# Two-block transformer, one core: layer norms computed with the tokens on the partitions

## The reference, cut to what matters

```python
for l in range(2):
    h = x @ w_in[l] + b_in[l]
    ...                                   # y_lru, y_nsa from h
    mix = concat([rms_norm(y_lru, gn_lru_g[l]), rms_norm(y_nsa, gn_nsa_g[l])]) @ w_out[l]
    x = layer_norm(ALPHA * x + mix, ln1_g[l], ln1_b[l])
    x = layer_norm(ALPHA * x + peer(x, ...), ln2_g[l], ln2_b[l])

def layer_norm(x, g, b):                  # over the 1024 features of a token
    mu = mean(x); var = mean((x - mu) ** 2)
    return (x - mu) * rsqrt(var + 1e-5) * g + b
```

## Time and profile before

| | us |
|---|---|
| median of 3 runs | 3153.09 (3152.42 to 3153.7) |
| the profiled execution | 3152.62 |
| its span, first to last instruction | 3150.8 |
| PE busy | 3091.8 (98%) |
| DVE busy | 2062.8 (65%) |
| ACT busy | 1442.4 (46%) |
| mean granted TensorE clock | 0.993 |
| PE's share of the chain that ended last | 94% |

### The profile page before, as it was taken

How to read it: one execution, slowest core, us unless ns; L and a number is a source line. 1 busy time by engine, 2 the same in 40 slices (tenths; PEclk the granted TensorE clock), 3 DMA queues, 4 the chain that set the end, 5 groups by cost and what they waited for, 6 DMA issues and landing times.

```text
span 3150.8 us, 46702 instructions
## 1 busy us (share of the span) xinstructions
PE 3091.8 (98%) x15882; PEld 2575.7 (82%) x15882; DVE 2062.8 (65%) x4058; ACT 1442.4 (46%) x2307; POOL 157.7 (5%) x289
## 2 busy tenths in 40 slices
PE   7999999999999999999999999999999999999998
PEld 6688876868887688899888888878889988888887
DVE  5567752636774352899776676665289976676676
ACT  2436642435663244156344544444415634544454
POOL 3100000200000000320000000000032000000000
PEclk9999999998999999999999999999999999999999
DMA  8748896734889632433655555644243265555663
GB/s 320 254 174 309 305 347 267 283 124 174 309 301 350 235 111 82 141 101 107 194 187 190 192 190 187 193 148 145 78 142 108 96 197 187 192 190 188 192 191 121
DMA packets 167140, 614.72 MB, mean 195 GB/s; under 512 B 18752, under 2 KB 18784, under 8 KB 166096
## 3 DMA queue, kind: packets, MB, share of 16 engines
q1 hardware_dynamic: 151632, 551.62, 51.4%
q0 software_dynamic: 15360, 61.16, 5.2%
HBM read 611.66 MB, written 1.05 MB: 194 GB/s over the span
## 4 chain that ended last, share of the span: by engine, by line
PE 94%; DVE 2%; ACT 2%; DMA 1%; issue 0%; DVEq 0%; POOL 0%; ACTq 0%; SPq 0%; POOLq 0%
PE PS L1639 13%; PE PS L1640 13%; PE PS L1641 13%; PE PS L2287 11%; PE PS L1685 7%; PE PS L2247 6%; PE PS L2289 6%; PE PS L2165 4%; PE PS L2270 4%; PE PS L1699 2%; PE PS L1726 2%; PE PS L1967 2%; PE PS L2153 2%; PE PS L2016 1%; PE PS L2279 1%; PE PS L1670 1%
## 5 line engine op out<-in xcount | busy, mean ns | idle before, releaser
L1016 DVE TENSOR_TENSOR w_lo<-arena,w_hi 128x1024 fp32r<-128x1024 f32 x448 | 530.2, 1220 | 0.0
L610 ACT ACTIVATE w_hi<-arena 128x1024 fp32r<-128x1024 f32 x448 | 451.5, 1048 | 97.3 <-DMA arena<-in_v_t 76.0
L1639 PE MATMUL PS<-w_hi,pw_hi 128*128 128x512 f32 x1024 | 402.1, 393 | 2.8 <-DVE w_lo L1016 2.3
L1640 PE MATMUL PS<-w_lo,pw_hi 128*128 128x512 f32 x1024 | 401.2, 392 | 0.0
L1641 PE MATMUL PS<-w_hi,pw_lo 128*128 128x512 f32 x1024 | 398.9, 390 | 0.0
L2287 PE MATMUL PS<-x_lh,w_hi 128*128 128x512 f32 x1536 | 379.5, 389 | 0.0
L2287 PEld LDWEIGHTS PS<-x_lh,w_hi 128*128 128x128 f32 x1536 | 288.3, 188 | 59.6
L956 ACT ACTIVATE arena<-PS 128x256 f32<-128x256 f32 x192 | 73.9, 385 | 446.8 <-PE PS L2289 446.8
L1237 DVE TENSOR_TENSOR gu_lo<-raw,gu_hi 128x1024 fp32r<-128x1024 f32 x192 | 222.6, 1221 | 19.2 <-ACT gu_hi L698 19.1
L1641 PEld LDWEIGHTS PS<-w_hi,pw_lo 128*128 128x128 f32 x1024 | 192.5, 188 | 41.4
L1639 PEld LDWEIGHTS PS<-w_hi,pw_hi 128*128 128x128 f32 x1024 | 193.1, 189 | 38.7 <-issue 2.6
(11 more groups left out here) (417 smaller groups left out, 5319.0 us busy)
## 6 DMA issues: line engine op xcount, KB each, us to landing
arena<-in_u_t SPq DMA_DIRECT2D x256, 512.0 KB, 4.5
arena<-in_v_t SPq DMA_DIRECT2D x256, 512.0 KB, 3.6
raw<-in_w_gu SPq DMA_DIRECT2D x192, 512.0 KB, 5.4
arena<-in_w SPq DMA_DIRECT2D x152, 512.0 KB, 3.6
arena<-in_w_ada POOLq DMA_DIRECT2D x96, 512.0 KB, 7.1
raw<-in_w_down SPq DMA_DIRECT2D x96, 512.0 KB, 5.6
arena<-in_w_gu SPq DMA_DIRECT2D x64, 512.0 KB, 7.4
arena<-in_w_down SPq DMA_DIRECT2D x32, 512.0 KB, 5.0
```

Of the source, the lines that this page charges most:

```text
L610: A(w_hi[:, m % RING], ring[:, m % RING], ACT.Copy).then_inc(S["hi_done"], 1)
L1016: V.tensor_tensor(w_lo[:, m % RING], ring[:, m % RING], w_hi[:, m % RING].bitcast(F32), ALU.subtract)\
L1639: mm(dst, w[0], m[0], start=start, stop=False)
L1640: mm(dst, w[0], m[1], start=False, stop=False)
```

## The change

The residual is no longer added by DVE. PE turns `x` (16 transposes, `residual`) into the four banks before the products are accumulated on top of it: in NSA eight of them before the first half of the projection and eight after the wait for the second half of `mix`, in PEER all before the first `down`. So that the sum is x + y / ALPHA, what is added is scaled by 1 / ALPHA: in NSA by a bias of the Exp that makes the rms factors, in PEER by a scale of the copy of the gates; the epsilon becomes 1e-5 / ALPHA**2. In NSA the projection's operands change places: `mix` (128 tokens) is stationary and the weight slot (128 output features) moves, so that both blocks leave tokens on the partitions. DVE then reads each bank with `bn_stats`, combines with `bn_aggr`, ACT takes a square root, DVE the reciprocal and one `tensor_scalar` per bank (subtract, multiply) into `y`; PE turns `y` with 16 transposes (`normed`) and ACT applies gain and bias out of the banks. The diff, cut (comments at the side say which engine's program it is; lines in brackets sum up lines left out):

```diff
-LN_BANK = (6, 0)
+LN_TURN = ((6, 7, 4, 5), (4, 5, 6, 7))
...
-        L_ = area([("sq", (KT, T)), ("rs", (T,)), ("y", (TT, D))], 16384)
+        L_ = area([("y", (TT, D))], 16384)
+        ln_st = sb("ln_st", [P, TT, 12])
+        ln_mv = sb("ln_mv", [P, TT, 4])
+        def ln_bank(q, t, half):
+            return 2 * t + half if q else OUT_BANK[2 * half + t]
...
             def layer_norm(l, q):                                   # ScalarE
-                for j in range(4):
-                    act.wait_ge(S["ln_c"], 4 * LN[s] + j + 1)
-                    A(L_["sq"][:, 2 * j:2 * j + 2], x[:, 2 * j:2 * j + 2], ACT.Square).then_inc(S["norm_sq"], 1)
-                root(s, L_["rs"], LN_BANK[q] + 1, LN_EPS)
+                A(ln_mv[:, 0, 2:3], ones[:, 0:1], ACT.Sqrt)
+                act.wait_ge(S["ln_var"], LN[s] + 1)
+                A(ln_mv[:, :, 1], ln_mv[:, :, 1], ACT.Sqrt, bias=LN_EPS / ALPHA ** 2).then_inc(S["ln_rs"], 1)
                 for k in range(KT):
-                    act.wait_ge(S["scaled"], KT * SIDX[s] + k + 1)
-                    A(x[:, k], x[:, k], ACT.Identity, scale=..., bias=...)
+                    act.wait_ge(S["ln_t"], KT // 2 * LN[s] + k // 2 + 1)
+                    A(x[:, k], PS[:, LN_TURN[q][k // 2], T * (k % 2):T * (k % 2) + T], ACT.Identity, scale=..., bias=...)
...
-                    A(..., ACT.Exp, scale=-0.5).then_inc(S["g_rs"], 1)
+                    A(..., ACT.Exp, scale=-0.5, bias=-math.log(ALPHA)).then_inc(S["g_rs"], 1)
...
-                A(gT, PS[:, 1, 0:T], ACT.Copy)
+                A(gT, PS[:, 1, 0:T], ACT.Copy, scale=1.0 / ALPHA)
...
-                act.wait_ge(S["slot_done"], BASE_SPLIT["peer", l] + PEER_SLOTS)
-                for q in range(2):
-                    for t in range(TT):
-                        last = A(L_["y"][:, t, 512 * q:512 * q + 512], PS[:, 2 * t + q, :], ACT.Copy)
-                    last.then_inc(S["y2_ev"], 1)
...
             def layer_norm(l, q):                                   # VectorE
-                dve.wait_ge(S["ln_mu"], LN[s] + 1)
-                for j in range(4):
-                    V.scalar_tensor_tensor(x[:, 2 * j:2 * j + 2], PS[:, LN_BANK[q], 0:T]...broadcast, -1.0 / D, x[:, ...], ALU.mult, ALU.add)
-                dve.wait_ge(S["norm_rs"], SIDX[s] + 1)
-                for k in range(KT):
-                    V.tensor_tensor(x[:, k], x[:, k], L_["rs"], ALU.mult).then_inc(S["scaled"], 1)
+                order = ((0, 0), (0, 1), (1, 0), (1, 1)) if q else ((0, 0), (1, 0), (0, 1), (1, 1))
+                for i, (t, half) in enumerate(order):
+                    if q and i < 3:
+                        dve.wait_ge(S["ln_z"], 5 * l + 2 + i + 1)
+                    elif q:
+                        dve.wait_ge(S["slot_done"], BASE_SPLIT[s] + PEER_SLOTS)
+                    elif t == 0:
+                        dve.wait_ge(S["ln_z"], 5 * l + half + 1)
+                    else:
+                        dve.wait_ge(S["slot_done"], BASE[s] + W2_IN + 4 * half + 4)
+                    V.bn_stats(ln_st[:, t, 6 * half:6 * half + 6], PS[:, ln_bank(q, t, half), :])
+                    if half:
+                        dve.drain()
+                        last = V.bn_aggr(ln_mv[:, t, 0:2], ln_st[:, t])
+                last.then_inc(S["ln_var"], 1)
+                dve.wait_ge(S["ln_rs"], LN[s] + 1)
+                V.reciprocal(ln_mv[:, :, 3], ln_mv[:, :, 1])
+                dve.drain()
+                for half in range(2):
+                    for t in range(TT):
+                        V.tensor_scalar(L_["y"][:, t, 512 * half:512 * half + 512], PS[:, ln_bank(q, t, half), :],
+                                        ln_mv[:, t, 0:1], ln_mv[:, t, 3:4], ALU.subtract, ALU.mult).then_inc(S["ln_n"], 1)
+                if not q:
+                    dve.drain().then_inc(S["pair_evac"], 4)
...
-                for j in range(4):                                  # VectorE, nsa
-                    dve.wait_ge(S["slot_done"], n0 + W2_IN + 2 * j + 2)
-                    V.scalar_tensor_tensor(x[:, 2 * j:2 * j + 2], x[...], ALPHA, PS[:, OUT_BANK[j], :]..., ALU.mult, ALU.add)\
-                        .then_inc(S["pair_evac"], 1)
...
-                V.tensor_tensor(x[:], x_hi.bitcast(F32), x_lo.bitcast(F32), ALU.add)   # VectorE, peer
-                dve.drain()
-                for j in range(4):
-                    dve.wait_ge(S["y2t"], 4 * l + j + 1)
-                    V.scalar_tensor_tensor(x[...], x[...], ALPHA, PS[:, 4 + j, :]..., ALU.mult, ALU.add).then_inc(S["z2_ok"], 1)
...
-            def means(l, q, j):                                     # TensorE
-                (two 128x256 products of ones with x per call, into PS[:, LN_BANK[q], 0:T])
+            def residual(q, half):
+                for t in range(TT):
+                    for k in range(4 * half, 4 * half + 4):
+                        mm(PS[:, ln_bank(q, t, half), P * (k % 4):P * (k % 4) + P], x[:, k, P * t:P * t + P], ident,
+                           start=k % 4 == 0, stop=False, is_transpose=True, skip_group_check=True)
+            def normed(l, q):
+                filler(9, 7)
+                for k in range(KT):
+                    if k % 4 == 0:
+                        pe.wait_ge(S["ln_n"], 4 * LN[s] + 2 * (k // 4) + 2)
+                    for t in range(TT):
+                        c0 = T * (k % 2) + P * t
+                        last = nc.tensor.transpose(PS[:, LN_TURN[q][k // 2], c0:c0 + P], L_["y"][:, t, P * k:P * k + P], ident)
+                    if k % 2:
+                        last.then_inc(S["ln_t"], 1)
...
                 def out_half(i, c):
-                    for k in range(4 * c, 4 * c + 4):
-                        last = mm(PS[:, OUT_BANK[i // 2], T * (i % 2):T * (i % 2) + T], ring[:, n % RING, P * k:P * k + P], N["mix"][:, k],
-                                  start=k == 0 and i % 2 == 0, stop=k == KT - 1, skip_group_check=True)
+                    for t in range(TT):
+                        for k in range(4 * c, 4 * c + 4):
+                            last = mm(PS[:, ln_bank(0, t, i // 4), c0:c0 + P], N["mix"][:, k, P * t:P * t + P],
+                                      ring[:, n % RING, P * k:P * k + P], start=False, stop=..., skip_group_check=True)
+                        if c and t == 0 and i % 4 == 3:
+                            last.then_inc(S["ln_z"], 1)
...
                 heads(1, (0, 1))
+                residual(0, 0)
                 pe.wait_ge(S["mix2_ok"], 2 * l + 1)
...
                 pe.wait_ge(S["mix2_ok"], 2 * l + 2)
+                residual(0, 1)
                 for i in range(W2_OUT):
                     if i >= RING:
                         out_half(i, 0)
                     out_half(i, 1)
-                    if i % 2 and i > 1:
-                        means(l, 0, i // 2 - 1)
-                means(l, 0, 3)
-                for j in range(4):
-                    squares(("nsa", l), L_["sq"], j, LN_BANK[0] + 1)
-                filler(9, 2)
+                normed(l, 0)
...
-                def down(n, j, b, i=0, per=0, start=False, stop=False):
+                def down(n, j, b, i=0, per=0, stop=False):
                     (the last call signals ln_z after each of its first three banks; no call starts a bank)
+                pe.wait_ge(S["gelu_ok"], PK * l + EARLY - LATE)
+                residual(1, 0)
+                residual(1, 1)
                 for b in range(EARLY):
-                    down(n0 + b, b, b, start=b == 0)
+                    down(n0 + b, b, b)
...
                 down(n0 + PEER_SLOTS - 1, PEER_STEP - 1, PK - 1, stop=True)
-                (16 transposes of y into banks 4 to 7, means, squares, and for l = 0 nine fillers)
+                normed(l, 1)
```

More of the change, by code:

```diff
@@ L816, in rms @@
                     act.drain()
-                    A(N["rs"][:, T * q:T * q + T], N["rs"][:, T * q:T * q + T], ACT.Exp, scale=-0.5).then_inc(S["g_rs"], 1)
+                    A(N["rs"][:, T * q:T * q + T], N["rs"][:, T * q:T * q + T], ACT.Exp, scale=-0.5, bias=-math.log(ALPHA)).then_inc(S["g_rs"], 1)
                 evac(0)
@@ L1635, in _, with mm3 @@
             mm = nc.tensor.matmul
[L1637 to L1641, removed]
+            def mm3(dst, w, m, start, stop, skip=False):
+                mm(dst, w[0], m[0], start=start, stop=False, skip_group_check=skip)
+                mm(dst, w[0], m[1], start=False, stop=False, skip_group_check=skip)
+                return mm(dst, w[1], m[0], start=False, stop=stop, skip_group_check=skip)
             def filler(n, bank):
@@ L2151, in out_half @@
                     wait_slot(pe, n)
-                    for k in range(4 * c, 4 * c + 4):
-                        last = mm(PS[:, OUT_BANK[i // 2], T * (i % 2):T * (i % 2) + T], ring[:, n % RING, P * k:P * k + P], N["mix"][:, k],
-                                  start=k == 0 and i % 2 == 0, stop=k == KT - 1, skip_group_check=True)
+                    c0 = P * (i % 4)
```

(22 more changed lines are left out.)

25 lines of the change are left out of this document (4 added, 21 removed).

## The result

| | before | changed |
|---|---|---|
| median, us | 3152.76 (3150.21 to 3153.7, 4 runs) | 3126.41 (3122.49 to 3129.93, 4 runs) |
| ratio | | 0.9917, 95% interval 0.9900 to 0.9935 |
| span of the profiled execution | 3150.8 | 3124.8 |

The forecast was 3125 (3117 to 3136). The head of the changed page, to be read against the earlier trace rows: PE's busy time fell by 16 us, the span by 26. The other 10 us are waiting that went.

A forecast was written before the change was run, and what follows sets the result against it. PE, busy 3091.8 of 3150.8 us, was taken as the bound. PEER 0 8.75, PEER 1 9.1 and the NSA blocks 9.6 sum to 27.5 us off 3152.6: 3125 forecast, range 3117 to 3136.

The forecast's parts named there:

- The four gaps: At the four layer norms PE waits on a chain between engines; these gaps hold 55 us, 15.29 after the first PEER block.
- The end of the kernel: After the second PEER block, last product to last gain-and-bias tile: 7.6 us in place of 18.58; the store's 2.4 stays.
- T0: The end of the last product before a layer norm, from which the prediction timed the norm's steps.
- The upper bound of two passes: In the norms, `bn_stats` at 1.2 us apiece: 2.0 us more in each PEER, 0.85 in each NSA, 5.7 in all.
- Gain and bias: Behind each norm, ACT's eight tiles 0.49 us apart, no table load; PE never catches up, saving 0.4 us besides.
- The exchange: In NSA's projection, 128 records of 256 columns become 256 of 128, 0.111 us apart: 0.85 us more.
- Rivals 3 and 4: In the projection: records 0.125 us apart, 3132 us, 6%; or weight loads not covered, records 0.30 apart, 3222 us, 3%.
- NSA's stretch: Each NSA projection, its norm and the next block's start: 4.8 us less, twice 9.6.
- The weight slots: At the next block's start, weights were held to be no limit, SP's order and conditions being unchanged; no cost taken.
- rival 5: The next block waits for a slot or POOL load, so gaps don't shorten: 5.9 us slower up to no change; 3%.
- the last sign of being wrong: PE idling on a weight slot where it now idles on the norm; no size given.
- rival 1: After the gaps PE's clock falls to half rate for 7 us: 3.5 us at each of three, 3136 us; 7%.

The follow-up runs named there:

- `a_split`: The changed kernel with the normalising pass shared: DVE takes token tile 0, ACT token tile 1; 3124.79 us in one run, gap 4.5 us (5.5).
- `a_res2`: The changed kernel with every group of residual transposes run twice; 3133.57 us in one run.
- `a_noex`: The changed kernel with the projection's operands not exchanged (weight slot stationary again, output wrong); 3126.68 us in one run.
- `a_first`: The changed kernel with all three of POOL's loads in NSA held back until the block's first weight slot is used; 3120.72 us, ratio to before 0.9903.
- `a_nofill`: The changed kernel without the nine filler products in each layer norm; 3131.12 us, ratio to before 0.9934.

## Why the prediction was right, and where it was off

- **The four gaps.** Right in mechanism and nearly in size. After PEER 0 5.05 was forecast and 5.5 measured. The term that was mis-sized is the normalising pass. The prediction took 0.62 us a pass from DVE's adds (2.48 us for four, which is 0.60 apart and 0.68 for one); measured are 2.96 us for four, 0.72 apart and 0.80 for one. The pass has two scalars of a column each, and the row that it was read from has none; that this is the reason was not tested. `a_split` shows that this pass is what sets the gap.
- **The end of the kernel**, 7.6 us forecast and 7.66 measured to the last tile, is two misses that cancel: the first turned tiles reached ACT 0.35 us later than forecast (T0 + 3.90, not 3.55), and the eight gain-and-bias tiles took 3.76 us and not 4.04.
- **`bn_stats`**, which no row had: 0.68 taken, 0.70 measured (0.65 at its shortest). Two of four are hidden and the third nearly, and the fourth ends at T0 + 0.79 where 0.71 was forecast. One `bn_aggr` 0.21 for 0.18. The upper bound of two passes did not come.
- **Gain and bias** came 0.45 apart, faster than 0.49, without a table load. PE had no wait in it, and of the 0.4 us hoped for 0.15 and 0.4 show in the two stretches PEER a.
- **The residual**: 1.9 forecast, 1.8 measured in PEER, exposed; `a_res2` confirms it.
- **The exchange**: 0.111 forecast and 0.112 measured apart, and 0.85 forecast and 0.9 measured a block (`a_noex`). Rivals 3 and 4 fell: with 256 loads of 0.19 us in each projection, the 512 records lie 0.1117 apart, 4 ns over half of the 0.216 of a 256-column record. By the rule of the Trainium skill, "TensorE: Matmul & The Clock Gate", section "Back-to-back issue gap", that rival 3 names, they would have lain some 25 ns further apart than the columns ask, an estimate; for these float32 products the trace disagrees with it.
- **NSA's stretch** fell by 4.2 us, and with what PEER a gained behind it by 4.4 and 4.6, where 4.8 was forecast: the normalising pass again.
- **The weight slots**: this step failed. The prediction said "The next block's weights are no limit ... SP's order and conditions are unchanged" and priced POOL's earlier start at nothing. The order within SP was unchanged; the order between SP's and POOL's loads was not. NSA 1 took 2.0 us more, where 0.4 less was forecast, and `a_first` shows the cause by taking 2.5 away. It was of rival 5's kind in one block, at a fraction of its price, and close to the last sign of being wrong that the prediction named, though PE idled on the slots 14 us behind the norm and not in it.
- **The clock** stayed up, against rival 1. `a_nofill` shows that the fillers, of which the prediction said only that they cost nothing, are what kept it up in two of three gaps.

The sum: forecast 27.5, by the stretches 24.0. Of the 3.5 between, 2.4 are in NSA 1 with its slots, 0.5 in the gap after PEER 0, and 0.6 in the two NSA norms with what follows them. That the first comparison of medians gave 26.4 fits the variation of the part that the change left alone, which was 2.1 us shorter in the profiled run. The total agreed with the forecast better than its terms did, and that much is luck.

## What to carry to other kernels

A norm between two products costs what its chain of engines costs, not its work: turn the layout so that the statistics are read where the product leaves them, let all but the last bank's share lie beside the product, and split the last full pass over two engines. When a stall goes, look at what the next stage's transfers waited for: a load released by the end of the stall may now be issued ahead of the one that PE needs first, and holding it back by one slot puts it right. Read single stretches of the timeline, not totals, where the effect is smaller than the variation between runs.

## What the hardware showed that was not expected

- The order of issue decided 2.5 us, though the transfers sit in different queues. A slot of 512 KB issued 0.1 us behind the last of three large loads on POOL's queue got no packet for 3.9 us and landed after 10.7, with the second of the three. Issued 0.55 us ahead of the first, it landed after 3.9. While both queues had work, the DMA engines took as many packets from one as from the other, 162 and 160 in 6 us, and as POOL's were larger (1.89 MB against 0.60), the slots got a quarter of some 420 GB/s.
- A pass of 512 columns from PSUM took 0.80 us on DVE with two column scalars, and 0.68 with a second tensor as operand.
- The clock fell in two of three like gaps without fillers, for 3.4 and 6.8 us; the third had the same 3.1 us of idle and kept it. Why was not tested.
